# A planner's durations, a charge for tile shapes and a path rule in the second stage of a two-layer kernel

## The reference

```python
p = rmsnorm(x, norm_g) @ w_in
# branch 1: a recurrence with a 64x64 state in each of 8 heads
S = S * w_t + sa[..., None] * (kk_t * a_t) + v_t[..., None] * k_t;  y_t = S @ r_t
# branch 2: attention over the 256 best of the earlier tokens, 8 heads
score = einsum('bqh,bqhs->bqs', w_i, relu(einsum('bqhd,bsd->bqhs', q_idx, k_idx)))
_, idx = lax.top_k(where(causal, score, -inf), 256)
o_lat = softmax(q_abs @ c_sel.T) @ c_sel                  # c_sel = c_kv[idx]
y = concat([y_rwkv * silu(g_rwkv), (o_lat @ w_uv) * silu(g_attn)]) @ w_out
```

## Time and profile before

| what | before |
|---|---|
| median of three runs | 4040.66 us |
| the profiled execution | 4036.41 us |
| its span, first to last instruction | 4034.6 us |
| TensorE busy in the span | 3735.2 us (93%) |
| last product of the first phase | 812 us |
| second phase on TensorE | 826 to 1942 us |

### The profile page before, as it was taken

One profiled execution on the slowest core, in us unless ns is written; L12 is line 12 of the kernel. 1 busy time (PEld: TensorE's weight loads), 2 busy tenths in 40 slices (PEclk: granted clock), 3 DMA queues, 4 the chain that ended last, 5 costly groups with the idle time before them and its releaser, 6 DMA issues. The chain is left out here.

```text
span 4034.6 us, 77419 instructions
## 1 busy us (share of the span) xinstructions
PE 3735.2 (93%) x31244; PEld 2724.5 (68%) x31244; DVE 2733.6 (68%) x5210; ACT 2074.9 (51%) x3093; POOL 1353.6 (34%) x1087
## 2 busy tenths in 40 slices
PE   6999989889888988889898999989999999999899
PEld 5777757757677777777686878765555555555577
DVE  5577678878877888888753332566777777777654
ACT  4354688858688878866433222323333333333432
POOL 2132123233564545554111000004544544545300
PEclk9999999999999999999899999999999999999899
DMA  3244223364533434344665344873322322331432
GB/s 123 84 133 154 69 93 106 117 219 132 147 89 109 127 117 124 95 114 147 188 214 203 118 141 146 274 229 63 87 62 59 82 59 58 85 66 30 139 116 75
DMA packets 419077, 483.40 MB, mean 120 GB/s; under 512 B 121312, under 2 KB 302048, under 8 KB 418464
## 3 DMA queue, kind: packets, MB, share of 16 engines
q1 hardware_dynamic: 417600, 475.01, 40.2%
q10 hardware_dynamic: 1120, 3.45, 0.3%
HBM read 319.04 MB, written 159.29 MB: 119 GB/s over the span
## 5 line engine op out<-in xcount | busy, mean ns | idle before, releaser
L150 ACT ACTIVATE PT<-psum 128x1024 f32<-128x1024 f32 x384 | 394.2, 1027 | 647.8 <-PE psum L140 647.2
L178 DVE TENSOR_REDUCE m<-psum 128x1 f32<-128x1024 f32 x384 | 468.7, 1222 | 280.0 <-PE psum L140 279.9
L140 PE MATMUL psum<-xc,wah 128*128 128x512 f32 x1600 | 529.6, 413 | 14.6 <-DVE xc L154 7.7
L154 POOL TENSOR_TENSOR part<-PT 128x1024 f32<-128x1024 f32 x144 | 341.1, 2369 | 475.5 <-DVE all L154 385.5
L140 PE MATMUL psum<-PT,V 128*64 128x512 f32 x1536 | 371.9, 605 | 0.0
L140 PEld LDWEIGHTS psum<-xc,wah 128*128 128x128 f32 x1600 | 302.5, 193 | 93.3 <-issue 21.6
L154 POOL TENSOR_TENSOR Lm<-gm,cst 64x512 f32<-64x512 f32 x192 | 261.7, 1363 | 305.9 <-DVE gm L154 164.6
L140 PE MATMUL psum<-xc,wal 128*128 128x512 f32 x800 | 318.6, 398 | 0.0
L151 ACT ACTIVATE bias<-score,cand,cols 128x2048 bf16<-128x2048 f32 (+4 forms) x155 | 244.5, 1577 | 64.3 <-DVE cand L161 61.5
L151 ACT ACTIVATE sgn<-score,cand,cols 128x1920 bf16<-128x1920 f32 (+4 forms) x155 | 227.9, 1470 | 63.0 <-DVE cand L161 59.9
L140 PE MATMUL psum<-hc,w4h 128*128 128x512 f32 x800 | 251.8, 400 | 7.8 <-DVE w4l L154 7.8
(11 more groups left out here) (424 smaller groups left out, 8978.9 us busy)
## 6 DMA issues: line engine op xcount, KB each, us to landing
ks<-scr_keys SPq DMA_DIRECT2D x112, 512.0 KB, 4.2
raw_a<-in_w_a SPq DMA_DIRECT2D x50, 512.0 KB, 3.9
raw_w<-in_w_in SPq DMA_DIRECT2D x32, 512.0 KB, 5.1
QNh<-scr_qnh SPq DMA_DIRECT2D x48, 256.0 KB, 5.0
QRh<-scr_qrh SPq DMA_DIRECT2D x192, 64.0 KB, 3.9
QNl<-scr_qnl SPq DMA_DIRECT2D x48, 256.0 KB, 5.3
xin<-in_x SPq DMA_DIRECT2D x16, 512.0 KB, 3.7
scr_AR<-AR SPq DMA_DIRECT2D x32, 256.0 KB, 2.4
```

Source lines behind the costliest of these rows:

```text
L140: return self.e.matmul(out, a, b, start=start, stop=stop, skip_group_check=True)
L150: return self.e.activation(out, src, f, bias=bias, scale=scale)
L154: return self.e.tensor_tensor(out, a, b, op) if self.e else self.vector(out)
L178: return self.e.tensor_reduce(out, a, AX, op, negate=negate) if self.e else self.vector(a)
```

## The change

The recorder now notes four numbers for an instruction: the old duration, which the other phases' planning still uses, a time for which it holds its engine, a time until its result has landed, and for TensorE a form: whether it has at most 64 rows, and at most 64 columns of weights. With `by_path=True`, which only the second phase's order has, `settle` uses the new numbers, adds 0.15 us whenever TensorE's form changes in place of 0.12 us at every piece, lets a DMA land after 4.5 us, counts waits inside a piece, and chooses anew: among the pieces that an engine could start within 0.1 us of coming free, TensorE takes one that keeps its form, if there is one, and beyond that every engine takes the one with the longest chain of pieces behind it (`paths`). No instruction is added or taken away.

```diff
     def vector(self, ap, fixed=0.15, slope=0.00105):
...
-        return self.idle(max(0.22, fixed + slope * each(ap)))
+        return self.idle(max(0.22, fixed + slope * each(ap)), None, fixed + slope * each(ap) - 0.085, fixed + slope * each(ap))
...
-        return self.e.dma_start(out, src) if self.e else self.idle(0.1, "dma")
+        return self.e.dma_start(out, src) if self.e else self.idle(0.1, "dma", 0.1, 4.5)
...
+            form = (a.shape[0] <= 64, each(a) <= 64)
+            rows = 2 if form[0] else 1
+            part = rows * (2 if form[1] else 1)
+            hold = max(0.109, 0.00044 * each(b)) / rows if a.dtype == FR else 2 * max(0.109, 0.00084 * each(b)) / part
...
     def tt(self, out, a, b, op):
+        if not self.e and self.name == "pool" and op == ALU.pow:
+            return self.idle(0.25 + 0.002 * each(out), None, 1.35, 1.4)
...
+    def paths(self, lanes):
...
+                    length[(e, k)] = max(hold, land) + 0.08
+                    follow[(e, k)] = [(e, x[n - 1][0])] if n else []
...
+                        if y[0] == "wait" and owner.get(y[1], (e, k)) != (e, k):
+                            follow[owner[y[1]]].append((e, k))
...
+                    rest[at] = length[at] + max([rest.get(x, 0.0) for x in follow[at]], default=0.0)
...
-                        if own is None or (go, place[k]) < own[:2]:
-                            own = (go, place[k], e, name)
-                if own and (best is None or own[:2] < best[:2]):
+                        rank = (go, place[k])
+                        if self.by_path:
+                            other = e == "pe" and self.form_of(items) not in (None, form)
+                            rank = (max(go, free[e] + 0.1), (10.0 if other else 0.0) - rest[(e, k)])
+                        if own is None or rank < own[0]:
+                            own = (rank, go, e, name)
+                if own and (best is None or (own[1], own[0][1]) < (best[1], best[0][1])):
                     best = own
...
-            if e == "pe":
+            if e == "pe" and not self.by_path:
                 t += 0.12
             for y in items:
-                if y[0] == "op":
+                if self.by_path:
...
+                        if y[5] and y[5] != form:
+                            form = y[5]
+                            t += 0.15
...
-        turns_2 = Order(order_2, lane_2, [bank[i] for i in (4, 5, 6, 0, 1, 2, 7, 3)])
+        turns_2 = Order(order_2, lane_2, [bank[i] for i in (4, 5, 6, 0, 1, 2, 7, 3)], by_path=True)
```

More of the change, by code:

```diff
@@ L122, in claim, with idle @@
         return order.banks_of(k, len(frees), self)
-    def idle(self, us, table=None):
-        self.book.note("op", us, table)
+    def idle(self, us, table=None, hold=None, land=None, form=None):
+        self.book.note("op", us, table, us if hold is None else hold, us if land is None else land, form)
         return Nothing()
@@ L147, in act @@
             table = {ACT.Sqrt: "root", ACT.Exp: "exp", ACT.Tanh: "exp"}.get(f)
-            return self.idle(0.1 + 0.00098 * each(out) + (0.19 if acc is not None else 0.0), table)
+            land = 0.15 + 0.00084 * each(out) + (0.41 if acc is not None else 0.0)
+            return self.idle(0.1 + 0.00098 * each(out) + (0.19 if acc is not None else 0.0), table, land - (0.19 if acc is not None else 0.1), land)
         if acc is None:
@@ L218, in of, with form_of @@
         return self.by.get(engine, self.pieces)
+    def paths(self, lanes):
+        follow, owner, length = {}, {}, {}
+        for e in lanes:
+            for x in lanes[e].values():
+                for n, (k, items) in enumerate(x):
+                    hold = land = 0.0
+                    for y in items:
+                        if y[0] == "op":
+                            land = max(land, hold + y[4])
+                            hold += y[3]
+                        elif y[0] == "up":
+                            owner[y[1]] = (e, k)
+                    length[(e, k)] = max(hold, land) + 0.08
+                    follow[(e, k)] = [(e, x[n - 1][0])] if n else []
+        for e in lanes:
+            for x in lanes[e].values():
+                for k, items in x:
+                    for y in items:
+                        if y[0] == "wait" and owner.get(y[1], (e, k)) != (e, k):
+                            follow[owner[y[1]]].append((e, k))
+        rest, seen = {}, set()
+        for first in length:
+            if first in seen:
+                continue
+            seen.add(first)
+            stack = [(first, iter(follow[first]))]
+            while stack:
+                at, others = stack[-1]
+                other = next((x for x in others if x not in seen), None)
+                if other is not None:
+                    seen.add(other)
+                    stack.append((other, iter(follow[other])))
+                else:
+                    rest[at] = length[at] + max([rest.get(x, 0.0) for x in follow[at]], default=0.0)
+                    stack.pop()
+        return rest
+    def form_of(self, items):
+        return next((y[5] for y in items if y[0] == "op" and y[5]), None)
     def settle(self):
```

25 lines of the change are left out of this document (19 added, 6 removed).

## The result

| | before | after |
|---|---|---|
| median | 4040.66 us (4035.21 to 4041.17, 5 runs) | 4055.39 us (4054.85 to 4058.13, 5 runs) |
| ratio to before, 95% interval | 1 | 1.0042 (1.003 to 1.0053) |
| span of the profiled execution | 4034.6 us | 4053.0 us |
| second phase on TensorE, first key tile to last product | 825.9 to 1941.8, 1115.9 us | 824.4 to 1958.4, 1134.1 us |

The changed kernel is 0.42% slower; the forecast was 1% faster. Between the two profiled executions the span grew by 18.4 us and the second phase by 18.2, so everything lies in it. (By the medians the loss is 14.7 us: the profiled execution of before took 4.25 us less than its median.)

What follows compares the result with a forecast made beforehand. It took TensorE as the second phase's bound, not by much. Terms -30 - 12 + 0 + 2 + 0 = -40 us from the profiled 4036.41 gave 3996.4, by the median 4000.7, said as 4000; own range 3975 to 4022, 8 in 10 3945 to 4052.

Steps and rivals of the forecast that it cites:

- Where the charges were wrong: Second phase's plan: corrected GpSimd power and 4.5 us DMA landing; effects counted in the -12 and +16 of TensorE's waits.
- Waits of TensorE: Second phase's handovers to TensorE: a tenth of 120 us idle goes, -12 us, between -60 and +16.
- Changes of form: TensorE's order in the second phase: 201 fewer changes, 877 to 676, at 0.15 us each, -30 us.
- TensorE is not the bound: Rival, second phase: other engines and PSUM banks set the pace, saved changes become waits; 4040 us, chance 0.15.
- The lower clock: TensorE at 1.2 GHz after long waits in the second phase: held at 0 us, between -16 and +4.
- The phase's start: 28 key and value tiles ahead of the first `log`, first search 29 us later: +2 us, from 0 to +8.
- late search: Rival, second phase: the first search's 29 us delay lasts to the tail and TensorE waits; 4060 us, chance 0.15.
- Searches and tail: ScalarE's search steps, 20 us more waits covered by spare time, and the phase's last short pieces: 0 us each.
- VectorE later than planned: Rival, second phase: sums with all inputs in SBUF undercharged by 26 us, all reaching TensorE; 4027 us, chance 0.08.

Runs made afterwards that it cites:

- dma_issue: Changed kernel with the plan holding the queue 0.62 us at every DMA in place of 0.1, landing still 4.5 us: 4031.12 us, ratio 0.9984.
- lds: Changed kernel with the load of bonus and gate moved from the loads' lane to the norm's on SP: 4040.39 us, ratio 1.0009.
- dma7: Changed kernel with the plan letting a DMA land after 7.0 us again in place of 4.5: 4087.82 us, ratio 1.0117.
- head: Changed kernel with the pieces up to block 4's last `log` kept in the woven list's order: 4021.25 us, ratio 0.9958.
- no_form: Changed kernel without TensorE's preference for a piece of its form, a piece chosen by its chain alone: 4051.69 us, ratio 1.0035.
- iss_head_nf: Changed kernel with the edits of dma_issue and head together, without TensorE's preference for a piece of its form: 4038.12 us, ratio 1.0005.
- search: Changed kernel with pieces of a search chosen ahead of everything else on every engine: 4080.83 us, ratio 1.0109.

## Why the prediction was wrong

**Where the charges were wrong: the step that failed.** It took the landing of a DMA from the key loads' 4.2 us and concluded that a score might wait a microsecond or so. Scores hardly wait for keys. The load that matters consists of seven DMAs, and its reader lies on the recurrence's chain. Its price was to be read from the trace of before, from the seven issues in 4.35 us and the landing 6.0 to 7.4 us after the first, against the plan's 5.1. What hid the old plan's equally wrong 0.1 us per issue was the list's order, which left over 10 us between landing and product in most units; the path rule takes that away. Measured: 38 us of new waits, of which at most 27 are the short charge itself, and 24 us of time by dma_issue, more than the 15 by which the kernel is slower. A second part of these waits is that the path rule lets the loads stand behind `lds` (lds, dma7). Mending the charge is enough to turn the sign; that nothing else would is not shown, since head turns it with the charge left as it is.

**Waits of TensorE.** -12 taken, bounds -60 to +16; measured +34.6. Without the step above it is +7.7 (dma_issue), inside the bounds and on the worse side of zero. The count of short covers looked at copies, sums, masks and states, and so left out the one handover that changed most. Its mark of 1.5 us was wide, too: in the trace of before, copies of 512 columns for which VectorE or ScalarE stood ready were back 0.73 and 0.64 us after the end of their product. The 6.8 us for GpSimd's power became 2.9, as said.

**Changes of form.** The mechanism was right and the size somewhat too large: 0.10 to 0.13 us measured for the 0.15 read, so 20 to 26 us for the 201 changes. Two things took it back. In the changed kernel it is hidden (no_form); in the repaired one about half of it counts (iss_head_nf). The rival that TensorE is not the bound was right about this term. "TensorEngine Tiling (Array Packing)" of the Trainium skill, section "Performance Considerations", names the emptying of PSUM as what may bind then: waits for ScalarE's copies of `Y` and `pt` did grow by 17 us, and without the preference for a form (no_form) they are 11.5 and 5.0 us, but VectorE's copies improved by 10 us, so the page's rule is one part of it and not the largest.

**The lower clock**. 0 taken, -16 to +4 allowed. The time at 1.2 GHz grew from 82 to 131 us, worth at most 24 us of busy time, and 8 by the line through all kernels; both are beyond the +4. Waits of over 4 us behind the first tile, two in before (9.1 us together), are eight after (42.3 us). By the same line the forms save 23 us, so 15 are left; measured 15.6.

**The phase's start.** The 29 us came out exactly (863.03 to 892.04), in part by luck: the first `log` goes 24.9 us later (829.25 to 854.13) and the last one of block 4 23.5 us later (850.02 to 873.53), and another 5.5 us are lost between it and the first Sign. The wait for the first tile stayed as said (13.5 to 13.3). +2 was too little, but not by much: with the loads repaired, the late start costs 2.4 to 9.1 us. The rival *late search* gave 4060 and the time was 4055; that is a coincidence of size. Half of its mark is in the trace, the last bias 18.3 us later; the other half, TensorE waiting for that bias ahead of block 13, is not, and dma_issue starts its search as late and is 24 us faster. There the last Sign ends 5 us earlier than in the kernel before: the 18 us by which the last search is late after are gone with the waits for `wu`.

**Searches and tail.** Both costed at 0. The tail was right: from the last bias to the last product it is 42.2 us before and 40.5 after. ScalarE, busy for 861 of 1135 us, had room for the 20 us more of waits between steps; that they cost nothing no run shows by itself.

**VectorE later than planned.** The two groups with all inputs in SBUF took 94.7 us together, for 89.1 before. TensorE's waits for VectorE's copies of `pt` fell by 10 us, so this rival's 26 us are not seen there; no run charges these sums rightly, and the rival is not tested.

What stays open is some 10 to 16 us. Orders that differ from the changed kernel by one number or rule of the plan lie 25 to 32 us behind it in ways that neither theory gave (dma7, search). And head alone gained 34 us, where 18 to 24 are explained: 15 by its 24.8 us less of load waits, at dma_issue's rate of 24 us for 39, and 2 to 9 by the earlier search. As any edit redraws the whole order, the times by themselves can't rule chance out; what they rest on is that dma_issue moved the one row that it was meant to move, while the four next ones (`Y`, `sm`, `DVE wu`, `ACT pt`) stayed within 5 us. The forecast's 4000 was not reached by any order: the best keeps 121.6 us of idle time and a mean clock of 0.95.

## What to carry to other kernels

A planner's error is harmless as long as its rule leaves slack, and becomes a stall when a new rule uses all the slack it believes in; so when a plan is made tighter, check each charge against the slowest kind of that operation in the trace, and for loads count the issues of the whole group on the queue and not the landing of one. Busy time saved on the fullest engine is worth something only as far as its waits do not grow: compare busy and idle time of the phase apart. An experiment on a planner redraws the whole order, so pair each edit with the row it is meant to move, and believe its time only if that row moved and the others stayed.

## What the runs showed of the hardware

The issue of a load is not free and not constant. Behind an idle queue, SyncE issued the seven loads of unit 15 of before in 4.35 us, 0.62 us each. Right behind six loads of weights the same seven took 9.4 us after, 1.3 us each. At unit 11 of the changed kernel, behind four more loads of the recurrence (start, length of the row):

```profile
1590.15 0.33 SPq L134 DMA_DIRECT2D ar<-scr_AR  x1
1590.53 2.69 SPq L134 DMA_DIRECT2D bk<-scr_BK  x3
1593.26 3.77 SPq L134 DMA_DIRECT2D bt<-scr_BT  x3
1597.07 3.82 SPq L134 DMA_DIRECT2D wu<-scr_VT  x4
1600.93 1.18 SPq L134 DMA_DIRECT2D ks<-scr_keys  x2
```

they took 7.67 us (1593.26 to 1600.93), 1.1 us each. So loads that stand close together on the queue came later, each of them. Whether the queue itself or the engines behind it set that pace no run here tells apart.
